# A product of constants in front of the last up-projection part of a two-block transformer kernel

## The chip, the cores and the metric

The kernel runs on one core of one Trainium2 chip. The metric is the device time of one execution in microseconds (us), from the first to the last instruction and a little around it. A program is run several times; the median stands for it.

## What is computed

256 tokens of width 2048 pass through two transformer blocks in float32. Only the second block's last half touches the change:

```python
# first block: stick-breaking attention, then a squared-ReLU MLP (2048 -> 8192 -> 2048)
# second block: chunked attention beside a multi-scale pool, then
h = rms_norm_2(x, pre_ffn_g[l])
up = causal_dwconv(h @ w_up[l], conv_w[l], conv_b[l])          # 2048 -> 2 x 5632
y = (jax.nn.gelu(up[..., :D_FF_2], approximate=True) * up[..., D_FF_2:]) @ w_down[l]
x = x + rms_norm_2(y, post_ffn_g[l])
```

All weight matrices are read once from memory (some 395 MB), and nearly all the work is their products with the 256 tokens.

## The kernel before

**Split operands.** Every float32 operand of a large product is held as two rounded halves, a high one and a low one (fp32r tiles): weights as `Wh` and `Wl`, activations as the first and the second 256 columns of a tile of `aHL`, `oHL1`, `oHL2`, `hid1` or `hid2`. A product is the sum high x high + high x low + low x high.

**Pieces and strips.** The weights come in 746 pieces of 256 rows by 512 columns (512 KB each). SP's queue loads a piece into one of six buffers of `raw`, ACT (ScalarE) rounds it into `Wh` (line 812), DVE (VectorE) makes `Wl = raw - Wh` (line 1024), both into rings of five buffers. Eight to twelve pieces that add up into the same PSUM banks are a strip. Two PSUM sets, `ps0` and `ps1`, of four banks of 512 columns take turns, one strip each.

**Two kinds of pieces**, by what stands still in the PE array (TensorE):

- Kind "T" (`feature_products`, line 1353) gives features by tokens. Weights stand, tokens move. For each of two weight row tiles and four banks it issues a pair: `Wh` against all 512 columns of the activation tile (its high and low halves), and `Wl` against the first 256. A piece is 8 pairs, 16 products, 8 x 768 = 6144 columns.
- Kind "N" (`row_products`, line 1341) gives tokens by features. Tokens stand, weights move. A piece is 12 products of 512 columns, 6144 columns too.

The queries, keys, both up-projections, the first block's output and down projections are T; the values, the second block's output and down projections are N.

**Order.** `plan_program` (line 53) writes one list of steps that all engines walk in order. `strip` (line 83) lists the pieces; `after` puts side jobs behind a certain piece. A step `products` is one piece. The second block's feed-forward runs in two parts, `c = 0` with six strips of each half of the up-projection and `c = 1` with five (loop at line 540): the part's up-projection strips (T), then its down projection `w_down_2` (N, four strips of 12 pieces in part 0 and of 10 in part 1). So part 1's up-projection, 10 strips or 80 pieces, follows directly on an N strip.

**Side products on PE** are few, in plain float32, and put in between pieces: column sums of squares (step `rms`, line 1397, one column each), and after them `spread` (line 1423), which multiplies the 128x128 tile `ones` with a 256-column diagonal tile to give a norm's factor as a row for each partition. ACT copies that row out of PSUM into `r_a` or `r_b` (line 840). Further there are the attention products, `mixed_tiles` (line 1478, sixteen 128-column products that scale and turn four tiles) and transposes. The last norm before the up-projection is `r6`; its row goes into `r_b` during part 0's second strip and is not written again. POOL (GpSimd) multiplies each up-projection strip by `r_b` (line 1314).

**The PE program** (line 1377): for a step `products` it waits for the strip's bank set, the activation tiles and the piece's `Wl` (`s_w_lo`), then issues the piece; every product is issued in `mm`, line 1336, so the profile gives nearly all of them this one line. The lines that are changed are in `strip`, in the loop at line 540 and in the branch at line 1386.

Of the kernel before, what the change touches and what calls it, by code (L numbers as in the profile page):

```python
# [11 lines left out]
TOK = 256  # L12
# [13 lines left out]
class Plan:  # L26
# [18 lines left out]
    def after(self, i, job, ahead=False):  # L45
        jobs = self.later_steps.setdefault(i, [])
        jobs.insert(0 if ahead else len(jobs), job)
# [5 lines left out]
def plan_program(sem):  # L53
    p = Plan(sem)
    step, done, after, later = p.step, p.done, p.after, p.later
    free = {n: [] for n in ("QK1", "T0", "T1", "E", "zs", "set0", "set1", "mT", "qk0", "qk1", "v0", "v1", "A0", "A1")}
    st = {}
# [25 lines left out]
    def strip(w, col, ks, mov, tiles, evac, kind="T", koff=0):  # L83
        first = len(p.pieces)
        for n, kp in enumerate(ks):
            src = (w, "rows", kp * 256, col)
            p.pieces.append(dict(src=src, shape=2, mov=mov, kt=2 * (kp - koff), tiles=tiles, kind=kind, first=n == 0,
                                 last=n == len(ks) - 1, evac=evac))
        return first


# [19 lines left out]
    def rms(name, col):  # L111
        s = side_set()
        total, mean, root = done("rms_total"), done("rms_mean"), done("rms_root")
        rec, sq, prod = done("rms_rec"), done("rms_rec"), done("rms_rec")
        r, diag = done("rms_r"), done("rms_diag")
        step("rms", set=s, col=col, need=st["total"], free=list(free[f"set{s}"]), ones=ones0, ident=ident,
             total=total, mean=mean, root=root, rec=rec, sq=sq, prod=prod, r=r, diag=diag)
        free["zs"], free[f"set{s}"] = [total], [mean]
        st[name + "c"] = r
        st["diag"] = diag  # L120
# [24 lines left out]
    def spread(name, row):  # L145
        s = side_set()
        turned, copied = done("row_turned"), done("row_copied")
        step("spread", set=s, row=row, diag=st["diag"], free=list(free[f"set{s}"]), turned=turned, copied=copied)
        free[f"set{s}"], free["zs"] = [copied], [turned]
        st[name] = copied  # L150

    def r_job(name, col, row):
        def f():
            rms(name, col)
            after(p.at + 1, lambda: spread(name, row), ahead=True)
        return f
# [115 lines left out]
    def evac_relu(t0):  # L272
        def f(s, k):
            summed, kw = common(s, k, free["T1"])
            relu, sq = done("relu_cut"), done("relu_squared")
            hi, lo = done("hid_hi"), done("hid_lo")
            step("relu", t0=t0, r=st["r2"], relu=relu, sq=sq, hi=hi, lo=lo, hid_free=[k], **kw)
            free["T0"], free["T1"] = [lo], [sq]
            hid_tiles[t0:t0 + 4] = [lo] * 4
        return f  # L280
# [11 lines left out]
    for c, n in enumerate((6, 5, 5)):  # L292
        for j in range(n):
            i = strip("mlp_w1", (at + j) * STRIP, ALL8, "aHL", tile_hl, evac_relu(4 * j))
# [156 lines left out]
    def evac_conv(j, which, t0):  # L451
        def f(s, k):
            summed, kw = common(s, k, free["T1"])
            step("sum", **kw)
            name = "E" if which else "zs"

            def scaled():
                u = done("conv_scaled")
                step("conv_scale", need=[summed, st["r6"]], done=u)
                free["T1"] = [u]  # L460
                later(1, lambda: newest(u))

            def newest(u):
                c = [done("conv_newest") for m in range(4)]
                step("conv_newest", which=which, j=j, need=[u, conv_in, *free[name]], c=c)
                free["T1"] = [c[3]]
                later(1, lambda: older(u, c, 0))
                later(2, lambda: older(u, c, 2))
                later(3, lambda: gated(st["older", which]))

            def older(u, c, m0):
                d1 = [done("conv_older") for m in range(2)]
                d2 = [done("conv_older") for m in range(2)]
                step("conv_older", which=which, j=j, m0=m0, c=c, d1=d1, d2=d2)
                st["older", which] = d2[1]
                free["T1"] = [d2[1], c[3]]

            def gated(c):
                if not which:
                    st["gelu"] = done("gelu")  # L480
                    step("gelu", need=c, done=st["gelu"])
                    return
                g = done("gated")
                step("gate", need=[c, st["gelu"]], done=g)
                free["zs"] = [g]

                def halves():
                    hi, lo = done("hid_hi"), done("hid_lo")
                    step("gate_halves", t0=t0, need=[g, k], hi=hi, lo=lo)
                    free["E"] = [lo]  # L490
                    hid_tiles[t0:t0 + 4] = [lo] * 4
                later(1, halves)
            later(0 if "r6" in st else 4, scaled)
        return f
# [45 lines left out]
    for c, n in enumerate((6, 5)):  # L540
        for j in range(n):
            for which in range(2):
                i = strip("w_up_2", which * 5632 + (at + j) * STRIP, ALL8, "aHL", tile_hl, evac_conv(at + j, which, 4 * j))
                if at + j + which == 0:
                    after(i + 10, r_job("r6", "b", "r_b"))
        for s4 in range(4):
            i = strip("w_down_2", s4 * STRIP, tuple(range(2 * at, 2 * (at + n))), "hid2", hid_tiles, evac_y(c, s4), kind="N",
                      koff=2 * at)
            if c == 1 and s4 == 0:
                after(i + 1, gain_rows)  # L550
                after(i + 6, turn_x3(0))
                after(i + 8, turn_x3(1))
                after(i + 12, lambda: step("ready_sqrt", need=None))
        at += n
# [49 lines left out]
    for i in range(N):  # L604
        q = p.pieces[i]
# [41 lines left out]
def build(nc, A, out):  # L647
    with ExitStack() as ctx:
# [14 lines left out]
        ones = sb("ones", [128, 128])  # L663
# [3 lines left out]
        r_b = sb("r_b", [128, TOK])  # L667
# [50 lines left out]
        p = plan_program(lambda name: ctx.enter_context(nc.semaphore(name)))  # L718
# [615 lines left out]
        def tensor_program(e):  # L1334
            def mm(o, l, r, start, stop):
                return e.matmul(o, l, r, start=start, stop=stop, skip_group_check=True)  # L1336
# [16 lines left out]
            def feature_products(q, P, half=None):  # L1353

                wh, wl, mov, kt = Wh[:, q["n"] % NW, :], Wl[:, q["n"] % NW, :], movs[q["mov"]], q["kt"]
                for t in range(2):
                    if half:
                        e.wait_ge(*half[t])
                    x = mov[:, kt + t, :]
                    for m in range(4):  # L1360
                        c = slice(t * 512 + m * 128, t * 512 + (m + 1) * 128)
                        mm(P[:, m, :], wh[:, c], x, q["first"] and t == 0, False)
                        r = mm(P[:, m, 0:TOK], wl[:, c], x[:, 0:TOK], False, q["last"] and t == 1)
                return r
# [12 lines left out]
            for st in p.steps:  # L1377
                k = st["kind"]
                if k == "products":
                    q = pieces[st["i"]]  # L1380
                    P = ps[q["set"]]
                    for t in st["need"]:
                        e.wait_ge(*t)
                    if st["lo"] and not st["half"]:
                        e.wait_ge(*st["lo"])
                    if q["kind"] == "T":
                        feature_products(q, P, (st["half"], st["lo"]) if st["half"] else None).then_inc(p.mm, 1)
                    elif q["kind"] == "P":
                        group_products(q, P).then_inc(p.mm, 1)
                    else:  # L1390
                        for row in st["rows"]:
                            m = row_products(q, row, P)
                            if row == 0 and st["row0"]:
                                m.then_inc(p.row0, 1)
                            if row == 1:
                                m.then_inc(p.mm, 1)
                elif k == "rms":
                    P = ps[st["set"]]
# [7 lines left out]
                elif k == "rms_pair":  # L1406
                    P = ps[st["set"]]
# [20 lines left out]
                elif k == "sb_scores":  # L1428
                    g, P = st["g"], ps[st["set"]]
                    q, kk = qk[:, g % 2, 0, :, :], qk[:, g % 2, 1, :, :]  # L1430
# [7 lines left out]
                elif k == "sb_weights":  # L1438
                    g, P = st["g"], ps[st["set"]]
                    for t in st["need"]:  # L1440
                        e.wait_ge(*t)
                    for b, terms in enumerate((((tri_r, 0),), ((tri_r, 1), (ones_r, 2)), ((tri_r, 2),))):
                        for n, (l, at) in enumerate(terms):
                            c = slice(at * 512, (at + 1) * 512)
# [3 lines left out]
                elif k == "values":  # L1448
                    g, blk, P = st["g"], st["blk"], ps[st["set"]]
# [3 lines left out]
                    for h in range(4):  # L1453
                        c = slice(h * 128, (h + 1) * 128)
# [3 lines left out]
                elif k == "sm_scores":  # L1458
                    g, P = st["g"], ps[st["set"]]
                    q, kk = qk[:, g % 2, 0, :, :], qk[:, g % 2, 1, :, :]  # L1460
# [17 lines left out]
                elif k == "mixed_tiles":  # L1478
                    j0, b0, P = st["j0"], st["b0"], ps[st["set"]]
                    for t in st["need"]:  # L1480
                        e.wait_ge(*t)
                    for n, i in enumerate((0, 2)):
                        for a in range(2):
                            for t in range(2):
                                j = j0 + i + a
# [3 lines left out]
                elif k == "turn_x3":  # L1489
                    c = st["c"]  # L1490
# [63 lines left out]
```

## Time and profile before

| what | value |
|---|---|
| median of 3 runs | 2148.95 us (2148.35 to 2153.14) |
| the profiled execution's own time | 2148.78 us |
| its span, first to last instruction | 2147.0 us |
| PE busy | 2128.6 us, 99% |
| DVE busy | 1286.2 us, 60% |
| ACT busy | 1064.4 us, 50% |
| POOL busy | 242.2 us, 11% |
| read from memory | 395.55 MB, 185 GB/s over the span |

The profiled execution has 1.8 us outside its span. PE's records are of matmuls that overlap in the pipeline, so a busy PE is not PE at its peak: how fast it goes is read from the starts of its records, one after the other.

### The profile page before, as it was taken

What the parts mean: (1) busy time and instruction counts of PE and PEld (TensorE: products, weight loads), DVE (VectorE), ACT (ScalarE), POOL (GpSimd) and SP (SyncE); (2) the same over time, 40 slices, a digit from 0 to 9 for tenths busy, and PEclk for the clock granted to TensorE, in tenths of its full rate; (3) what the DMA queues carried; (4) which work ended last, traced back from release to release, by engine and by line L of the source; (5) the groups of instructions that cost most, each with busy time, mean ns of one, the idle gap of its engine ahead of it and who ended that gap; (6) DMA issues with size and microseconds to landing.
All of it is one profiled execution on the core that took longest, in us unless ns stands there. A gap on an engine that the chain in (4) does not pass through costs nothing.

```text
span 2147.0 us, 28153 instructions
## 1 busy us (share of the span) xinstructions
PE 2128.6 (99%) x11698; PEld 1848.7 (86%) x11698; DVE 1286.2 (60%) x1335; ACT 1064.4 (50%) x1198; POOL 242.2 (11%) x135
## 2 busy tenths in 40 slices
PE   8999999999999999999999999999999999999998
PEld 7888888888888888888888888888888888888886
DVE  6555556655555565565669655576666644566655
ACT  6554554545334443444554544455455433554553
POOL 3000001100000000000224000032222100222211
PEclk9999999999999999999999999999999999999999
DMA  8555555565656655665566555545665666566563
GB/s 279 162 174 174 177 166 187 177 205 167 211 191 183 196 185 192 177 205 189 191 193 193 178 175 181 182 148 179 193 196 177 215 193 189 167 187 202 191 199 113
DMA packets 207472, 399.50 MB, mean 186 GB/s; under 512 B 12400, under 2 KB 15600, under 8 KB 207088
## 3 DMA queue, kind: packets, MB, share of 16 engines
q1 hardware_dynamic: 207056, 395.60, 58.4%
q8 instruction: 92, 1.51, 0.3%
q10 hardware_dynamic: 288, 2.10, 0.3%
q14 instruction: 36, 0.29, 0.0%
HBM read 395.55 MB, written 2.10 MB: 185 GB/s over the span
## 4 chain that ended last, share of the span: by engine, by line
PE 98%; DVE 1%; ACT 0%; DMA 0%; issue 0%; SPq 0%; DVEq 0%; ACTq 0%
PE ps L1336 98%; DMA raw<-in_sb_w_qkv_dram 0%; PE ps L1339 0%; DVE raw L1234 0%; DVE Wl L1024 0%; DVE E L1063 0%; ACT E L862 0%; ACT E L860 0%; ACT T L958 0%; ACT zs L855 0%; DVE QK L1213 0%; ACT E L858 0%; ACT L860 0%; ACT Wh L812 0%; DVE aHL L1186 0%
## 5 line engine op out<-in xcount | busy, mean ns | idle before, releaser
L1024 DVE TENSOR_TENSOR Wl<-raw,Wh 128x1024 fp32r<-128x1024 f32 x745 | 920.4, 1256 | 618.0 <-ACT Wh L812 617.1
L1336 PE MATMUL ps<-aHL,Wh 128*128 128x512 f32 x3328 | 1164.4, 395 | 8.3 <-DVE Wl L1020 6.5
L812 ACT ACTIVATE Wh<-raw 128x1024 fp32r<-128x1024 f32 x745 | 768.6, 1054 | 608.3 <-PE ps L1336 602.9
L1336 PE MATMUL ps<-aHL,Wl 128*128 128x256 f32 x3328 | 931.9, 280 | 0.0
L1336 PEld LDWEIGHTS ps<-aHL,Wh 128*128 128x128 f32 x3328 | 624.7, 188 | 150.7 <-DVE aHL L1014 6.5
L1336 PEld LDWEIGHTS ps<-aHL,Wl 128*128 128x128 f32 x3328 | 629.7, 189 | 0.4
L1336 PE MATMUL ps<-hid,Wh 128*128 128x512 f32 x1024 | 355.1, 391 | 0.0
L1336 PE MATMUL ps<-hid,Wl 128*128 128x256 f32 x1024 | 286.9, 280 | 0.0
L1336 PEld LDWEIGHTS ps<-hid,Wh 128*128 128x128 f32 x1024 | 191.5, 187 | 41.9
L1336 PE MATMUL ps<-Wh,hid 128*128 128x512 f32 x704 | 217.6, 390 | 0.0
L1336 PEld LDWEIGHTS ps<-hid,Wl 128*128 128x128 f32 x1024 | 193.8, 189 | 0.0
L1336 PEld LDWEIGHTS ps<-Wh,hid 128*128 128x128 f32 x704 | 132.2, 188 | 27.4
L1336 PE MATMUL ps<-Wl,hid 128*128 128x512 f32 x352 | 137.0, 389 | 0.0
L1336 PE MATMUL ps<-Wh,aHL 128*128 128x512 f32 x384 | 121.4, 392 | 0.5 <-DVE Wl L1024 0.5
L1261 POOL TENSOR_TENSOR E<-E 128x512 f32<-128x512 f32 x8 | 10.4, 1305 | 943.4 <-ACT E L816 943.4
L1314 POOL TENSOR_TENSOR T<-T,r_b 128x1024 f32<-128x1024 f32 x22 | 71.0, 3229 | 400.2 <-DVE T L979 392.4
L979 DVE TENSOR_TENSOR T<-ps,T 128x1024 f32<-128x1024 f32 x54 | 66.1, 1224 | 56.3 <-ACT T L786 54.8
L1336 PE MATMUL ps<-oHL,Wh 128*128 128x512 f32 x272 | 94.6, 394 | 0.0
L786 ACT ACTIVATE T<-ps 128x1024 f32<-128x1024 f32 x54 | 55.2, 1022 | 68.5 <-PE ps L1336 68.5
L1336 PEld LDWEIGHTS ps<-Wh,aHL 128*128 128x128 f32 x384 | 72.1, 188 | 15.9 <-DVE Wl L1024 0.9
L1336 PE MATMUL ps<-Wh,oHL 128*128 128x512 f32 x256 | 79.6, 390 | 0.0
L1336 PEld LDWEIGHTS ps<-Wl,hid 128*128 128x128 f32 x352 | 66.1, 188 | 13.6
(171 smaller groups left out, 1290.4 us busy)
## 6 DMA issues: line engine op xcount, KB each, us to landing
raw<-in_mlp_w_dram SPq DMA_DIRECT2D x256, 512.0 KB, 4.3
raw<-in_w_up_dram SPq DMA_DIRECT2D x176, 512.0 KB, 3.9
raw<-in_sb_w_qkv_dram SPq DMA_DIRECT2D x95, 512.0 KB, 4.8
raw<-in_w_down_dram SPq DMA_DIRECT2D x88, 512.0 KB, 4.2
raw<-in_w_in_dram SPq DMA_DIRECT2D x64, 512.0 KB, 4.4
raw<-in_sb_w_o_dram SPq DMA_DIRECT2D x32, 512.0 KB, 4.4
raw<-in_w_o_dram SPq DMA_DIRECT2D x32, 512.0 KB, 4.0
xT<-in_x_dram SPq DMA_DIRECT2D x8, 256.0 KB, 7.9
```

The source lines that it names most:

```text
L786: e.activation(T0[:, :, :], ps[st["set"]][:, :, TOK:2 * TOK], ACT.Copy).then_inc(st["copied"][0], 1)
L812: e.activation(Wh[:, i % NW, :], rawv[:, i % NRAW, :], ACT.Copy).then_inc(st["hi"][0], 1)
L979: e.tensor_tensor(T1[:, :, :], ps[st["set"]][:, :, 0:TOK], T0[:, :, :], ALU.add).then_inc(st["summed"][0], 1)
L1024: e.tensor_tensor(Wl[:, i % NW, :], rawv[:, i % NRAW, :], Wh[:, i % NW, :].bitcast(F32), ALU.subtract).then_inc(st["lo"][0], 1)
L1261: e.tensor_tensor(B[:, 0:2, :], B[:, 0:2, :], B[:, 2:4, :], ALU.add).then_inc(st["half"][0], 1)
L1314: e.tensor_tensor(T1[:, :, :], T1[:, :, :], rows4("r_b"), ALU.mult).then_inc(st["done"][0], 1)
L1336: return e.matmul(o, l, r, start=start, stop=stop, skip_group_check=True)
```

## The change

In front of the first piece of part 1's first up-projection strip, PE gets one more product: `ones` (128x128, float32) stands, `r_b` (256 columns, float32) moves, and the result goes to the first 256 columns of bank 0 of the strip's own set. The next product, the strip's first, opens bank 0 anew, so the result is overwritten and nobody reads it. PE also waits there for `r6`, the copy of the factor row into `r_b`.

```diff
@@ strip
             p.pieces.append(dict(src=src, shape=2, mov=mov, kt=2 * (kp - koff), tiles=tiles, kind=kind, first=n == 0,
-                                 last=n == len(ks) - 1, evac=evac))
+                                 last=n == len(ks) - 1, evac=evac, wide=None))
@@ the loop over the parts of the up-projection
                 if at + j + which == 0:
                     after(i + 10, r_job("r6", "b", "r_b"))
+                if c == 1 and j + which == 0:
+                    p.pieces[i]["wide"] = lambda: st["r6"]
@@ tensor_program, step "products"
                     if q["kind"] == "T":
+                        if q["wide"]:
+                            e.wait_ge(*q["wide"]())
+                            mm(P[:, 0, 0:TOK], ones[:, :], r_b[:, :], True, True)
                         feature_products(q, P, (st["half"], st["lo"]) if st["half"] else None).then_inc(p.mm, 1)
```

On PE, where part 0's last down-projection strip (weights `Wh`, `Wl` moving against `hid2`) meets part 1's first up-projection strip (`aHL` moving), there stands before:

```order
9122 L1336 MATMUL ps<-Wl,hid 128x512
9123 L1336 MATMUL ps<-Wh,hid 128x512
9124 L1336 MATMUL ps<-aHL,Wh 128x512
9125 L1336 MATMUL ps<-aHL,Wl 128x256
9126 L1336 MATMUL ps<-aHL,Wh 128x512
```

and with the change, at the same place:

```order
9122 L1338 MATMUL ps<-Wl,hid 128x512
9123 L1338 MATMUL ps<-Wh,hid 128x512
9124 L1338 MATMUL ps<-r_b,ones 128x256
9125 L1338 MATMUL ps<-aHL,Wh 128x512
9126 L1338 MATMUL ps<-aHL,Wl 128x256
```

One row is added and all later ones stand one place further; nothing changes place, on PE or on another engine.

## Rows read from the trace of the kernel before

**Rows 1.** The page: busy time of the engines, PE's granted clock, the chain's shares.

```profile
PE 2128.6 (99%) x11698; PEld 1848.7 (86%) x11698; DVE 1286.2 (60%) x1335; ACT 1064.4 (50%) x1198; POOL 242.2 (11%) x135
...
PEclk9999999999999999999999999999999999999999
...
PE 98%; DVE 1%; ACT 0%; DMA 0%; issue 0%; SPq 0%; DVEq 0%; ACTq 0%
```

**Rows 2.** Who PE waited for from 1390 us on: total us, times, longest us.

```profile
PE ps L1336 <- DVE aHL L1186: 1.3, 1, 1.3
```

**Rows 3.** Stretches: us, PE busy (x records), granted clock, DMA share, GB/s.

```profile
1798.76:2024.88 226.12, 226.12 (x1281) 1.00 0.59 183
...
411.08:1118.05 706.97, 706.97 (x4081) 1.00 0.60 189
...
1435.43:1668.16 232.73, 232.73 (x1344) 1.00 0.60 187
1668.16:1798.76 130.60, 130.60 (x578) 1.00 0.64 201
```

**Rows 4.** PE in order of time at 1798.5 us: start us, us, what.

```profile
1798.54 0.39 PE L1336 MATMUL ps<-Wh,hid 128*128 128x512 f32 x1
1798.76 0.39 PE L1336 MATMUL ps<-aHL,Wh 128*128 128x512 f32 x1
1798.99 0.28 PE L1336 MATMUL ps<-aHL,Wl 128*128 128x256 f32 x1
1799.11 0.40 PE L1336 MATMUL ps<-aHL,Wh 128*128 128x512 f32 x1
1799.34 0.28 PE L1336 MATMUL ps<-aHL,Wl 128*128 128x256 f32 x1
1799.45 0.40 PE L1336 MATMUL ps<-aHL,Wh 128*128 128x512 f32 x1
1799.70 0.28 PE L1336 MATMUL ps<-aHL,Wl 128*128 128x256 f32 x1
1799.82 0.40 PE L1336 MATMUL ps<-aHL,Wh 128*128 128x512 f32 x1
```

**Rows 5.** Shorter stretches of T products, by what stands in front.

```profile
79.90:82.71 2.81, 2.81 (x17) 1.00 0.73 214
1224.77:1227.59 2.82, 2.82 (x18) 1.00 0.88 252
1229.13:1237.36 8.23, 8.23 (x48) 1.00 0.57 161
1409.16:1431.54 22.38, 22.38 (x128) 1.00 0.49 141
1240.21:1273.27 33.06, 33.06 (x193) 1.00 0.60 178
52.05:54.59 2.54, 2.54 (x16) 1.00 0.69 202
...
1125.69:1200.34 74.65, 74.65 (x433) 1.00 0.66 196
...
1119.18:1124.59 5.41, 5.41 (x32) 1.00 0.86 293
```

**Rows 6.** PE in order of time at the last `spread`, 1434.8 us.

```profile
1434.77 0.59 PE L1336 MATMUL ps<-zs,ones 128*128 128x256 f32 x2
1435.01 0.59 PE L1336 MATMUL ps<-aHL,Wh 128*128 128x512 f32 x1
1435.43 0.28 PE L1336 MATMUL ps<-aHL,Wl 128*128 128x256 f32 x1
1435.55 0.39 PE L1336 MATMUL ps<-aHL,Wh 128*128 128x512 f32 x1
1435.78 0.28 PE L1336 MATMUL ps<-aHL,Wl 128*128 128x256 f32 x1
```

**Rows 7.** Tile `r_b`: ACT's copies into it, ns min/median/max, first and last start.

```profile
L840 ACT ACTIVATE r_b<-ps x2: 384/384/384, 411.0 to 1435.4; 128x256 f32<-128x256 f32 x2
```

## The prediction

> **What bounds the kernel now.** I read the page first. PE is busy 99% of the span, the clock it is granted is at the upper of its two levels (2.4 GHz) in all slices, 9 meaning 90% or more, and 98% of the chain that ended last is PE [rows 1]. So a microsecond added to PE's stream or taken from it is a microsecond of the kernel, and nothing else matters unless it makes PE wait. The waits come next: from 1390 us to the end PE waited for another engine once, for 1.3 us, at the start of the up-projection [rows 2]. In the last part PE waits for nobody. What is left to look at is how fast PE's own stream goes when nothing holds it.
>
> For that I cut the trace into stretches in which PE does one kind of piece, with the bounds on the starts of records [rows 3]. A record that is still running at a bound is counted too, so I take the number of products from the program. The last up-projection part is 80 pieces of 8 pairs (512 columns, then 256): 640 pairs in 226.12 us, **353.3 ns a pair**. The up-projection of the part before goes from 1435.43 (the 256-column half of a first pair, 0.12 us) to 1668.16: 671 further pairs in 232.73 - 0.12 = 232.61 us, **346.7 ns a pair**. The long stretch of the first block from 411.08 gives 2039 pairs in 706.85 us, again 346.7 ns. These are the same products on the same tiles, at the same granted clock (1.00), with the same DMA share (0.59 and 0.60), and PE has no gap in either. The same work has two paces, 6.6 ns a pair apart. The starts show what the slow one looks like [rows 4]: from one 512-column product to the next it takes 0.35, 0.34 (or 0.35) and 0.37 us, and so on in threes (1798.76, 1799.11, 1799.45, 1799.82). In the fast one a pair is 0.35 us (its partners at 1435.43 and 1435.78 [rows 6]), and by the mean no long one can come in between.
>
> What chooses the pace? I looked at what PE does right in front of each run of T pieces [rows 5], where a window that opens on a 256-column start has 0.12 us taken off:
>
> - N pieces directly in front: 8 pairs in 2.81 us from 79.90 and 8 in 2.82 us from 1224.77, so 351 and 352 ns, and 353.3 ns over the 640 pairs of the stretch in question, whose first product follows on an N product 0.22 us before [rows 4]. Three other places, at the later query strips of the first block, look like the one at 79.90. The slow pace in 6 of 6.
> - a row `spread` in front (256 columns in plain float32): 7 pairs in 2.42 us from 52.05, 346 ns; 215 pairs in 74.53 us from 1125.69, 346.7 ns; and the two long stretches of [rows 3], 346.7 ns. The fast pace in 4 of 4, also where the T pieces ahead were in the slow pace: 15 pairs in 5.29 us from 1119.18 to the row products before 1125.69, 353 ns.
> - short float32 products in front give either: after transposes 23 pairs in 8.11 us from 1229.13, 353 ns; after `mixed_tiles` 63 pairs in 22.26 us from 1409.16, 353 ns; but after attention values 95 pairs in 32.94 us from 1240.21, 346.7 ns.
>
> No pace changes within a run, the longest being 2040 pairs. So the pace is a steady pattern that the entry picks and that then holds till something else comes between. I read it as a matter of how far the weight loads are ahead of the products when the alternation of 512 and 256 columns begins; a long product in front lets them get ahead. That is a reading, the counts above are what the sum rests on.
>
> **The change part by part.**
>
> 1. *The added product.* It has the form of `spread`: `ones` standing, 256 float32 columns moving. There its two records start at 1434.77, the next T product at 1435.01, and that one's partner at 1435.43 [rows 6]. From the float32 product's start to the partner's start are 0.66 us; without it there would be the usual 0.23 us from a 512-column product to its partner (1435.55 to 1435.78). Price: 0.66 - 0.23 = **0.43 us**, all of it on the path, as PE has no gap here. Bounds: the product can't cost less than nothing. Above, the side work nearest in kind that costs more for its width is the same product's own whole 0.66 us, if nothing of it overlapped. I take 0.43, since form, width and follower are the same; only what is ahead (an N product here, a T product there) and the bank (the follower's own here, another there) differ. The T pairs themselves write one bank twice in a row in every pair, without showing a gap.
> 2. *The added wait.* It is for a copy into `r_b` that was done at 1435.8 [rows 7], more than 360 us before the place. Nothing, and nothing else is queued differently. What is behind it on PE is the whole rest of the program, so I name the cover: it is the 363 us.
> 3. *The pace of the 640 pairs behind it.* At the fast pace they take 640 x 0.3467 = 221.9 us in place of 226.12: **4.24 us less**. The lower bound is no change, 0; the upper bound is this whole difference, since no long stretch of T pieces in the trace is faster than 346.7 ns a pair. I take all of it, because all four 256-column float32 products lead into the fast pace and no stretch in it fell back.
> 4. *What is late next.* Nothing new: the part before ran at the fast pace with the same work on DVE, ACT and POOL and the same loads, and PE did not wait. The down projection behind it is N, 48 pieces in 130.60 us in part 0 [rows 3], 226.7 ns for each of its 576 products; it comes 3.8 us earlier and takes the same time.
>
> Sum: 0.43 - 4.24 = -3.8 us. Against the profiled execution's own 2148.78 us that is 2145.0 us. This execution lies 0.17 us under the median of the runs; from the median it is 2148.95 - 3.8 = **2145.1 us**, 0.18% less. A measurement of this kernel can tell about 0.2% from no change, which is 4.3 us, so the forecast lies just inside that.
>
> Here a rule of the Trainium skill speaks against the change. The trace's row is that the same pairs take 353.3 ns in one stretch and 346.7 in another [rows 3]. The page "TensorE: Matmul & The Clock Gate", section "Wait — 56ns, not 53.3ns?", says that once the array is warm a matmul costs its columns at 2.4 GHz and a fixed 2.5 ns or so, whatever came before it; by it a pair is one number, an estimated 325 ns, there is no pace to choose, and the sum is the added product alone. The trace disagrees with the fixed part: both paces are above it, and they differ from each other.
>
> **The rivals.**
>
> *A. The pace stays slow and the product is only paid for.* The wide product stands behind an N stream here, and in all four cases of the trace behind T pieces, which already alternate. If the pace is set by something that the N stream leaves behind (or by nothing that a single product changes), the 640 pairs stay at 353.3 ns. For it: short float32 products between T pieces leave the slow pace in place twice [rows 5]. Against it: the row products before 1125.69, which turned a slow stretch into a fast one, so a wide product does act on the pattern; and the attention values, which have 256-column products too, lead to the fast pace. Time: 2148.95 + 0.43 = **2149.4 us**, slower than before. It decides from the point at which the gain is under the price: 0.43 us over 640 pairs is 0.7 ns, so if the pair stays above 352.6 ns the change loses. This is also what the page's rule named above would give.
>
> *B. The fast pace comes, but is lost on the way.* At the starts of pieces PE has waits for `Wl`, and a late one could bring the slow pattern back. Against it: three stretches of 215, 671 and 2039 pairs at the fast pace never fell back. If it is lost half way, the gain is 2.1 us less the price, **2147.3 us**.
>
> *C. The change doesn't do what it says.* The instruction stands in PE's stream exactly once and in front of the right strip, so only a product that is shortened away by the hardware would do; nothing in the trace hints at that. Nothing for it beyond what A gives.
>
> **How the numbers follow.** Forecast 0.81, A 0.14, B 0.05. The forecast's own spread is that of medians of a few runs: 2148.35 and 2148.95 are 0.6 us apart, and one of the three runs was 4.2 us above, as much as one such stretch in the other pace, so a median may move by half a microsecond: 2144.3 to 2145.9. To hold 8 in 10 the range has to take in A, with the same slack: 2144.2 to 2149.7. For the signs the bound is 2144.65. The forecast misses it by 0.5 us; I give it a chance of 0.31 that the measurement falls beyond, so faster by over 0.2% is 0.81 x 0.31 = 0.25. Slower by over 0.2% needs a median that caught a disturbed run, 0.04. The rest, 0.71, is within 0.2%.
>
> **What would show it.** In the profile after, two records `r_b,ones` of 256 columns stand at about 1798.8 us, and the first pair's 256-column product starts 0.66 us behind their start. The stretch of T products from there to the first down-projection product is about 222.3 us long in all, in place of 226.12, and the starts of its 512-column products have no third pair of 0.37 us. The last down projection starts at about 2021.1 us in place of 2024.88. PE has no new wait. Everything before 1798 us is as it was. The prediction is wrong if the pairs stay at 353 ns (A), if the first pair comes more than 0.7 us after the product, or if another stretch changes its pace.

## The result and the profile after

| | before | with the change |
|---|---|---|
| median | 2148.98 us (22 runs) | 2145.1 us (22 runs) |
| lowest and highest | 2147.58 to 2154.05 | 2143.79 to 2149.83 |
| ratio, 95% interval | | 0.9982 [0.9976, 0.9988] |

The change gains 3.9 us, 0.18%, where 3.8 us and a time of 2145.1 us were forecast. The profiled execution of the changed kernel doesn't show this gain in its span, because it is one of two among the 22 that lie 4 to 5 us above the rest: it took 2149.53 us, with a span of 2147.8 us. The kernel before has such executions too, four of its 22, from 2152.28 to 2154.05 us.

The page of the kernel after, its span, busy times, granted clock and the chain's shares, answering to [rows 1]:

```profile
span 2147.8 us, 28157 instructions
...
PE 2129.4 (99%) x11700; PEld 1849.0 (86%) x11700; DVE 1285.9 (60%) x1335; ACT 1064.6 (50%) x1198; POOL 241.4 (11%) x135
...
PEclk9999999999999999999999999999999999999999
...
PE 98%; DVE 1%; ACT 0%; DMA 0%; issue 0%; SPq 0%; DVEq 0%; ACTq 0%
```

There are two records more on PE (one float32 product is two) and two weight loads, and else the picture is the same. PE's waits from 1390 us on, as in [rows 2]:

```profile
PE ps L1338 <- DVE aHL L1188: 1.3, 1, 1.3
```

The added wait costs nothing. Now PE in order of time at the added product, kernel after (start us, us, what), to be held against [rows 4] and [rows 6]:

```profile
1803.12 0.39 PE L1338 MATMUL ps<-Wh,hid 128*128 128x512 f32 x1
1803.35 0.59 PE L1338 MATMUL ps<-r_b,ones 128*128 128x256 f32 x2
1803.59 0.59 PE L1338 MATMUL ps<-aHL,Wh 128*128 128x512 f32 x1
1804.01 0.28 PE L1338 MATMUL ps<-aHL,Wl 128*128 128x256 f32 x1
1804.13 0.39 PE L1338 MATMUL ps<-aHL,Wh 128*128 128x512 f32 x1
1804.36 0.28 PE L1338 MATMUL ps<-aHL,Wl 128*128 128x256 f32 x1
1804.48 0.39 PE L1338 MATMUL ps<-aHL,Wh 128*128 128x512 f32 x1
```

From the product's start to the first partner's are 0.66 us, as at the row product of before, and behind it a pair takes 0.35 us. The stretches of the kernel after (us, PE busy, granted clock, DMA share, GB/s), answering to [rows 3]: part 1 from the added product on, the same from the first partner on, part 0 from its first partner on, and part 0's down projection:

```profile
1803.35:2025.65 222.30, 222.30 (x1284) 1.00 0.57 185
1804.01:2025.65 221.64, 221.64 (x1281) 1.00 0.57 185
1435.55:1672.76 237.21, 237.21 (x1345) 1.00 0.57 185
1672.76:1803.35 130.59, 130.59 (x579) 1.00 0.61 200
```

Part 1 takes 222.30 us in place of 226.12: 3.8 us less. Without the first partner's 0.12 us, 639 pairs take 221.52 us, 346.7 ns each. But part 0, which the change does not touch, takes 237.21 us for what took 232.73 before: 671 pairs at 353.3 ns, the slow pace. That is 4.5 us more, and it is why this one execution is not shorter than the profiled one of before. So the trace shows two things at once: the mechanism that was forecast for part 1, and the reason why this execution lies above.

### The profile page after: what moved, and what is told of

It reads as the page before. It is cut to its first block, busy times and chain, and to the rows that moved or that the text cites. A ratio compares the mean times of both kernels' runs of the same rounds, so it can differ in the third digit from the quotient of the medians.

```text
span 2147.8 us, 28157 instructions
## 1 busy us (share of the span) xinstructions
PE 2129.4 (99%) x11700; PEld 1849.0 (86%) x11700; DVE 1285.9 (60%) x1335; ACT 1064.6 (50%) x1198; POOL 241.4 (11%) x135
## 4 chain that ended last, share of the span: by engine, by line
PE 98%; DVE 1%; ACT 0%; DMA 0%; issue 0%; SPq 0%; DVEq 0%; ACTq 0%
PE ps L1338 98%; DMA raw<-in_sb_w_qkv_dram 0%; PE ps L1341 0%; DVE raw L1236 0%; DVE Wl L1026 0%; DVE E L1065 0%; ACT E L864 0%; ACT E L862 0%; ACT T L960 0%; ACT zs L857 0%; DVE QK L1215 0%; ACT E L860 0%; ACT L862 0%; ACT Wh L814 0%; DVE aHL L1188 0%
```

## The experiments

Twelve runs on the chip. Each is the changed kernel with one thing different, unless it says otherwise. The pace in part 1 is read in every profile from the first partner's start to the first down-projection product. It came out as 221.64 or as 225.90 us each time that all 640 pairs were at one pace (225.89 us in the kernel before), never between: 346.7 or 353.3 ns a pair. The executions without a profile have only their time, and a slow part 0 and a slow part 1 each add some 4 us to it, so a single time 4 us above doesn't say which part was slow.

### The change again

> The change once more, for a second profile. Theory L (lead): the T products take the fast pace (346.7 ns a pair) if the weight loads are ahead of the products when the alternation of 512 and 256 columns begins, and a wide float32 product gives that lead unless its own weight load came late. L expects 346.7 ns over the 640 pairs behind the added product, a price of 0.43 us, and in the part before it (672 pairs from 1435 us) 346.7 ns if the row product's weight load was not held up, 353.3 if it was. A span of about 2143.4 us in the first case, 2147.8 in the second. Rival W (width alone): every 256-column float32 product leads into the fast pace; it expects 346.7 in both parts always. Rival D (drift): the pace is drawn at random at each entry; it expects either pace behind the added product in this profile.

Measured: 2145.06 us median (10 runs, 2144.57 to 2146.02), ratio 0.9979 [0.9969, 0.9989]. In this profile both parts have the fast pace, with a span of 2143.1 us (part 0 from its first partner, then part 1 from its own):

```profile
1435.29:1668.04 232.75, 232.75 (x1345) 1.00 0.57 188
1799.29:2020.93 221.64, 221.64 (x1281) 1.00 0.57 186
```

So the 4.5 us of the first profile come and go with part 0's pace, and the profile's span follows: 2147.8 - 2143.1 = 4.7 us. Rival W had fallen with the first profile already, whose part 0 is slow behind a product of 256 columns; D is not excluded by this one.

What was different at part 0's entry in the profile after? There the row product's weight load waited for the diagonal tile from DVE, which was ready late (weight loads of the kernel after: start us, us, what, idle before it and its releaser):

```profile
1434.43 0.19 PEld L1338 LDWEIGHTS ps<-aHL,Wl 128*128 128x128 f32 x1
1434.78 0.30 PEld L1338 LDWEIGHTS ps<-zs,ones 128*128 128x128 f32 x2 [0.16 <-DVE zs L998]
```

In the kernel before these two loads began 0.23 us apart, with no wait:

```profile
1434.42 0.19 PEld L1336 LDWEIGHTS ps<-aHL,Wl 128*128 128x128 f32 x1
1434.65 0.30 PEld L1336 LDWEIGHTS ps<-zs,ones 128*128 128x128 f32 x2
```

Theory L took that for the cause: a wide product gives the weight loads a lead unless its own load is late. But in this second profile the load was held up just so, and the fast pace came all the same:

```profile
1434.52 0.30 PEld L1338 LDWEIGHTS ps<-zs,ones 128*128 128x128 f32 x2 [0.16 <-DVE zs L998]
```

The other profiles say the same. Eleven of the fourteen, before and the experiments below included, have this load held up (the row product's two records start 0.30 to 0.32 us apart, in place of 0.22), and ten of these eleven have a fast part 0. L stood only on one case, and the next runs went for it at the added product.

### The product behind a drained pipeline, and the drain alone

```diff
                         if q["wide"]:
                             e.wait_ge(*q["wide"]())
+                            e.wait_ge(p.mm, q["n"])
                             mm(P[:, 0, 0:TOK], ones[:, :], r_b[:, :], True, True)
```

> The added product as in the change, but PE waits in front of it until its own last N product is complete, so that the added product's weight load starts late and in an empty pipeline. L: the lead is gone or smaller, the 640 pairs take 353.3 ns, and the time is before plus 0.43 us plus the drain of some 0.2 us. W: the width alone counts, 346.7 ns a pair, and the time is that of the change plus 0.2 us, 3.6 us under before. D: either.

Measured: 2145.83 us median (10 runs), ratio 0.9985 [0.9976, 0.9995]. PE in order of time:

```profile
1799.15 0.39 PE L1338 MATMUL ps<-Wh,hid 128*128 128x512 f32 x1
1799.69 0.67 PE L1338 MATMUL ps<-r_b,ones 128*128 128x256 f32 x2
1800.01 0.59 PE L1338 MATMUL ps<-aHL,Wh 128*128 128x512 f32 x1
1800.43 0.28 PE L1338 MATMUL ps<-aHL,Wl 128*128 128x256 f32 x1
```

Part 1 from the first partner on, as a stretch:

```profile
1800.43:2022.07 221.64, 221.64 (x1280) 1.00 0.57 185
```

The product starts 0.54 us behind the last N product in place of 0.23, so its load is late, and the pace is fast. L, as it was written, falls: a late load in front of the wide product does not bring the slow pace. Two of the ten executions lie above, at 2149.58 and 2150.27 us.

The second of the pair waits, and leaves the product out:

```diff
                         if q["wide"]:
-                            e.wait_ge(*q["wide"]())
-                            mm(P[:, 0, 0:TOK], ones[:, :], r_b[:, :], True, True)
+                            e.wait_ge(p.mm, q["n"])
```

> No added product; PE only waits in front of the strip until its last N product is complete. The drain alone costs about what it cost with the product, 2145.8 - 2145.1 = 0.8 us. If an empty pipeline is what resets the pattern, the 640 pairs take 346.7 ns and the time is 4.24 - 0.8 = 3.4 us under before; if it takes the wide float32 product (theory W, which the run with product and wait agreed with), 353.3 ns and 0.8 us over before.

Measured: 2147.65 us median, ratio 0.9990 [0.9981, 1.0000], which stands for nothing, as the ten runs fall into two heaps: 2145.04, 2145.52, 2145.56, 2145.82, 2146.07 and 2149.24, 2149.42, 2149.48, 2149.99, 2150.56. The profile is of the upper heap, with part 0 fast and part 1 slow:

```profile
1798.57 0.39 PE L1338 MATMUL ps<-Wh,hid 128*128 128x512 f32 x1
1799.10 0.47 PE L1338 MATMUL ps<-aHL,Wh 128*128 128x512 f32 x1
1799.41 0.28 PE L1338 MATMUL ps<-aHL,Wl 128*128 128x256 f32 x1
1799.53 0.40 PE L1338 MATMUL ps<-aHL,Wh 128*128 128x512 f32 x1
```

Its part 1 from the first partner on, as a stretch:

```profile
1799.41:2025.31 225.90, 225.90 (x1281) 1.00 0.56 183
```

Neither expectation was right: the same program takes either pace from one execution to the next. Of the upper five, the profiled one had part 1 slow; in the others it may have been part 0. The lower five, though, can only be executions in which part 1 was fast, without any added product: at the slow pace no execution of the kernel before was under 2147.2 us. A restart out of a drained pipeline leaves the choice open. With the product behind the same wait, part 1 was fast in the profile and in at least eight of the ten executions.

### Narrower, and rounded

One 128-column float32 product; one of 256 and one of 512 columns with rounded operands; two of 128; one of 192:

```diff
-                            mm(P[:, 0, 0:TOK], ones[:, :], r_b[:, :], True, True)
+                            mm(P[:, 0, 0:128], ones[:, :], r_b[:, 0:128], True, True)
@@ or, without the wait for r6
+                            mm(P[:, 0, 0:TOK], Wh[:, q["n"] % NW, 0:128], aHL[:, q["kt"], 0:TOK], True, True)
@@ or
+                            mm(P[:, 0, 0:2 * TOK], Wh[:, q["n"] % NW, 0:128], aHL[:, q["kt"], 0:2 * TOK], True, True)
@@ or the first of these lines twice, or with 192 for 128
```

> The added product with 128 columns in place of 256. Short float32 products led to either pace in the trace of before. L: the lead gained over two passes of 128 columns is half; if it is not enough, 353.3 ns a pair and a time of before plus 0.22 us; if enough, 346.7 ns, 0.2 us better than the change, 4.0 us under before. W: 353.3 ns, as the width is missing. A view in which any interruption of the N stream is enough: 346.7 ns.

> In place of the float32 product one of 256 columns with rounded operands (the piece's own Wh block standing, its activation tile moving), into the same bank, without the wait for the row; its sum is overwritten. Price about 0.12 us, one pass. L: a 256-column product of one pass leaves less time than a weight load, so no lead is won, 353.3 ns a pair, 0.1 us slower than before. A view in which only the order of 512 and 256 columns at the entry counts (the pattern starts on a 256 after the N stream): 346.7 ns and 4.1 us under before. W: 353.3 ns, as it is not float32.

> In place of the float32 product one of 512 columns with rounded operands (the piece's own Wh block standing, its whole activation tile moving), as wide in time as one float32 record of 256 columns, 0.22 us. W (float32, two records of two passes): 353.3 ns a pair, 0.2 us over before. If only the length of the record in front of the alternation counts, 346.7 ns and 4.0 us under before; but N products have that length too, and did not do it.

> Two float32 products of 128 columns, one behind the other, in place of one of 256: the same passes and columns in all, 0.43 us, but in records of half the length. If the whole float32 time in front counts: 346.7 ns a pair, first distance from the 512-column product to its partner about 0.42 us, and the time of the change. If the length of the last record counts: 353.3 ns, first distance about 0.31 us as with one of them, and 0.4 us over before.

> The two products of 128 columns once more, timed. The N stream in front has one distance for all its products (226 to 227 ns), so by F the state at this entry is the same in every execution and so is the pace: the fast one as in its profile, all executions at 2145 to 2146 us but for the 1 to 2 of 10 that part 0's entry puts 4 us above. If the pace were drawn at random here, as behind the drained pipeline of the run with the wait alone (5 of 10), about half would lie at 2149.5 us.

> The added product with 192 columns. F: one pace in all executions, which one is open; fast gives 2145.1 - 0.1 = 2145.0 us, slow 2148.95 + 0.3 = 2149.3 us. A view by width says that the limit lies between 128 and 256 columns; a view by the length of all float32 records in front (0.11 x 2 slow, 0.11 x 4 fast, 0.215 x 2 fast) says that it lies between 0.22 and 0.43 us, and 192 columns are 0.32.

| added in front of part 1 | part 1 from the first partner | time |
|---|---|---|
| nothing (before) | 225.89 us | 2149.10 to 2149.22 us beside these |
| 512 columns, rounded | 225.90 us | 2149.22 us (1 run) |
| 256 columns, rounded | 225.90 us | 2149.49 us, ratio 1.0002 [0.9993, 1.0012] |
| 128 columns, float32 | 225.90 us | 2149.47 us, ratio 1.0002 [0.9993, 1.0011] |
| 2 x 128 columns, float32 | 221.64 us, twice | 2145.25 us, ratio 0.9986 [0.9977, 0.9995]; an earlier single run 2147.29 us |
| 192 columns, float32 | 221.64 us | 2145.17 us, ratio 0.9979 [0.9970, 0.9989] |
| 256 columns, float32 | 221.64 us, twice | 2145.06 us, ratio 0.9979 [0.9969, 0.9989] |

The single run of two products of 128 columns, 2147.29 us, lies between the heaps for another reason. Both of its parts have the fast pace, but its granted clock over the first 50 us was 0.97 where it was 1.00 in the second profile of the change, and its part 1 starts 2.6 us later.

The edges of it in the trace, PE in order of time and then part 1 as a stretch: one product of 128 columns, two of them, and one of 192:

```profile
1799.10 0.38 PE L1338 MATMUL ps<-r_b,ones 128*128 128x128 f32 x2
1799.24 0.48 PE L1338 MATMUL ps<-aHL,Wh 128*128 128x512 f32 x1
1799.55 0.28 PE L1338 MATMUL ps<-aHL,Wl 128*128 128x256 f32 x1
...
1799.55:2025.45 225.90, 225.90 (x1280) 1.00 0.56 183
```

```profile
1801.09 0.60 PE L1338 MATMUL ps<-r_b,ones 128*128 128x128 f32 x4
1801.45 0.48 PE L1338 MATMUL ps<-aHL,Wh 128*128 128x512 f32 x1
1801.77 0.28 PE L1338 MATMUL ps<-aHL,Wl 128*128 128x256 f32 x1
...
1801.77:2023.41 221.64, 221.64 (x1280) 1.00 0.57 185
```

```profile
1799.63 0.49 PE L1338 MATMUL ps<-r_b,ones 128*128 128x192 f32 x2
1799.82 0.53 PE L1338 MATMUL ps<-aHL,Wh 128*128 128x512 f32 x1
1800.19 0.28 PE L1338 MATMUL ps<-aHL,Wl 128*128 128x256 f32 x1
...
1800.19:2021.83 221.64, 221.64 (x1280) 1.00 0.57 185
```

Not every interruption of the N stream will do, so the gain is not from the break as such, and neither of the two rounded products did anything. But the width of a single product is not the measure either: two of 128 columns bring the fast pace, and behind them the first pair looks as behind one (0.31 and 0.32 us to the partner). What goes with the outcome here is how much float32 work stands in front altogether. From the starts, up to the first partner and less its usual 0.23 us, it is 0.22 us with 128 columns (1799.10 to 1799.55), which is too little, 0.33 us with 192, 0.45 us with two of 128 and 0.43 us with 256, which are enough.

These runs don't separate the type from the length. The two rounded products took 0.11 and 0.22 us by the same reading, so neither was longer than the float32 product of 128 columns that did nothing either, and a longer run of rounded products was not tried here. The trace of before has one, which [rows 5] leave out: in the first block eight rounded products of the attention, 512 columns each, stand between T pieces in the slow pace (from 79.90 us) and further T pieces. The last of them, the first pair behind, and the 32 pairs up to the next side product as a stretch:

```profile
84.35 0.39 PE L1336 MATMUL ps<-E_lo,tri_r 128*128 128x512 f32 x1
84.58 0.40 PE L1336 MATMUL ps<-aHL,Wh 128*128 128x512 f32 x1
84.81 0.28 PE L1336 MATMUL ps<-aHL,Wl 128*128 128x256 f32 x1
...
84.58:95.67 11.09, 11.09 (x65) 1.00 0.72 233
```

That is 347 ns a pair, the fast pace, behind rounded products alone, and it is so at all four such places in all fourteen profiles. So float32 work is not needed for the fast pace; what sets these rounded products apart from the N pieces, behind which it was always the slow one, stays open.

In all of these that ran ten times the time has one heap and up to two of the ten executions some 4 us above it: 2153.38 and 2154.53 with 128 columns and 2153.36 and 2153.69 with 256 rounded ones, where part 1 is slow anyway, 2149.82 with two of 128, none with 192. With 128 columns or 256 rounded ones none of ten came near 2145 us, so part 1 was slow in every execution. With the others it was fast in at least 19 of 20. So behind an N stream, whose products start 0.22 to 0.23 us apart throughout, the entry left no choice that these runs show.

### Behind T pieces

```diff
-                if c == 1 and j + which == 0:
+                if c == 1 and j == 0 and which == 1:
```

> The added product one strip later, in front of part 1's second up-projection strip, so behind T pieces in the slow pace. The first strip's 64 pairs stay slow (0.42 us more than in the change), the 576 pairs behind should be fast: 2145.5 us. F: since T pieces in front leave the entry open by some ns, a few executions may stay slow here besides those of part 0, more than the 1 to 2 of 10 that lie 4 us above. W (the width alone counts): none more.

Measured: 2145.64 us median (10 runs, one at 2150.32), ratio 0.9986 [0.9977, 0.9995]. The first strip stays slow and the 575 pairs behind the product's first partner are fast, (199.46 - 0.12) / 575 = 346.7 ns:

```profile
1822.56:2022.02 199.46, 199.46 (x1153) 1.00 0.56 185
```

So the product turns a slow stretch into a fast one also from among T pieces. That more executions would stay slow was not seen: one of ten lies above, as with the change itself (two of 22).

### Part 0's entry

Two runs went for the executions that lie above. In the first the column sums for `r6` are made one piece earlier, with the row product in its old place, so that its operand is long ready:

```diff
-    def r_job(name, col, row):
+    def r_job(name, col, row, gap=1):
@@ in it
-            after(p.at + 1, lambda: spread(name, row), ahead=True)
+            after(p.at + gap, lambda: spread(name, row), ahead=True)
@@ the loop over the parts of the up-projection
                 if at + j + which == 0:
-                    after(i + 10, r_job("r6", "b", "r_b"))
+                    after(i + 9, r_job("r6", "b", "r_b", 2))
```

> The change, and the column sums for the factor r6 one piece earlier, its row product where it was, so that its operand has been ready for a piece's time. Theory L for the row product: the pace of the 672 pairs of part 0 is even (230 and 117 ns, 346.7 a pair) whenever the row product's weight load is not held up; the executions that lie 4 to 5 us above the rest (14 of 115 so far, over all kernels) are those in which it was held up and the pairs fell into the slow pace. Expected: in the profile the two float32 records at about 1434.7 us start 0.215 us apart (held up they were 0.32) and the first distance behind them is 0.425; among 16 executions none above 2148; the median as the change's, 2145.1. Rival: the outliers have another cause; then some 2 of 16 lie at 2149 to 2150 all the same.

Measured: 2145.80 us median, 11 runs (ratio 0.9982 [0.9973, 0.9991]), one of them at 2149.71. The two records were no longer held up (0.216 us apart), and yet the first distance, from the first T product to its partner, was 0.418 us and not the expected 0.425, and one execution still lies above. In this profile both parts are fast. PE also waited 1.0 us for the column sums, about the 0.7 us by which this version is slower than the change:

```profile
PE ps L1338 <- DVE T L981: 1.0, 1, 1.0
```

So the held-up load is not the cause, at least not alone. The second run issues the row product twice, for `r6` only:

```diff
@@ the step's entry
-        step("spread", set=s, row=row, diag=st["diag"], free=list(free[f"set{s}"]), turned=turned, copied=copied)
+        step("spread", set=s, row=row, twice=name == "r6", diag=st["diag"], free=list(free[f"set{s}"]), turned=turned, copied=copied)
@@ tensor_program, step "spread"
+                    if st["twice"]:
+                        mm(ps[st["set"]][:, 1, 0:TOK], ones[:, :], D, True, True)
                     mm(ps[st["set"]][:, 1, 0:TOK], ones[:, :], D, True, True).then_inc(st["turned"][0], 1)
```

> The change, and the row product for r6 (in part 0) issued twice, one behind the other, as the pair of row products at 1125 us is (two products, four records), which in all ten profiles so far was followed by a first distance of 0.425 us and the even pattern of 230 and 117 ns. Theory F (fixed state in, fixed pace out): which pace T products take is set by a few nanoseconds at the entry; behind T pieces, whose starts wander by some ns, a single row product leaves 0.417 to 0.426 us and now and then the slow pace, a doubled one always 0.425. F expects a price of 0.43 us, a median of 2145.1 + 0.4 = 2145.5 to 2146.0 us, and no execution 4 us above the rest (single: 1 to 2 of 10). Rival: the executions that lie above have nothing to do with this entry, and 1 to 3 of 17 lie at 2149 to 2151 all the same.

Measured: 2149.80 us median, 11 runs: 2145.43, 2145.96, 2145.97, and eight from 2149.54 to 2152.34. The opposite of what was expected. The profile is of the upper heap. PE at part 0's entry:

```profile
1434.69 1.02 PE L1338 MATMUL ps<-zs,ones 128*128 128x256 f32 x4
1435.37 0.58 PE L1338 MATMUL ps<-aHL,Wh 128*128 128x512 f32 x1
1435.79 0.28 PE L1338 MATMUL ps<-aHL,Wl 128*128 128x256 f32 x1
```

The two stretches of the same profile:

```profile
1804.27:2025.91 221.64, 221.64 (x1281) 1.00 0.57 185
1435.79:1672.98 237.19, 237.19 (x1344) 1.00 0.56 185
```

It shows that part 0's entry can fill the upper heap: an edit there alone moved it from 2 of 22 executions to 8 of 11, and the profile shows part 0 at 353.3 ns a pair, part 1 at 346.7. (The one at 2152.34 us lies higher still; no profile shows why.) It also refutes that more float32 work in front is always better: 0.87 us of it led to the slow pace here, while the same doubled form at 1125 us led to the fast one in all fourteen profiles. Nor does the first distance tell the pace, as this run's expectation had it: by the starts in the trace it was 0.418 us here and 0.420 in the profile after, both slow, and 0.418 in the run before this one and 0.419 in the second profile of the change, both fast.

## Why the prediction was right, point by point

- **Step 1, the product's price.** Taken as 0.66 - 0.23 = 0.43 us; in the profile after it is 1803.35 to 1804.01, again 0.66 us. That an N product stands ahead and that the bank is the follower's own made no difference that the trace shows.
- **Step 2, the wait.** No new wait of PE. Right.
- **Step 3, the pace.** 640 pairs at 346.7 ns were forecast, 346.7 measured in every profile with the product in it, and 222.30 us for the stretch where 222.3 were named. The median gained 3.9 us for a sum of 3.8.
- **Step 4, nothing late next.** The down projection's 130.60 us [rows 3] are 130.59 after, and PE does not wait.
- **The page's rule** (once the array is warm, a matmul in a back-to-back stream costs its columns and a fixed 2.5 ns or so: the Trainium skill, "TensorE: Matmul & The Clock Gate", section "Wait — 56ns, not 53.3ns?") leaves the pairs one pace, which is rival A, 2149.4 us. The runs decide against it for these pairs: the same 640 took 346.7 or 353.3 ns each, at a granted clock of 1.00.
- **Rival A** did not come, with 256 columns. With 128 columns and with 256 rounded ones it did, at 2149.5 us.
- **Rival B** was not seen: the part took 221.64 us or 225.90, nothing between.
- **Rival C** did not come: the two records of the product stand at 1803.35 us, as shown above.
- **The signs.** One of the prediction's own signs of being wrong came: in the profile after, another stretch, part 0, changed its pace, and with it the places named moved; the last down projection starts at 2025.65 us there in place of the forecast 2021.1. In the second profile, with part 0 fast, it starts at 2020.93. The median is right because part 0, by the times, stayed fast in most executions of both kernels.

What was wrong is beside the sum. First, the evidence for step 3, "four 256-column float32 products lead into the fast pace", was read from one execution of before and is no rule behind T pieces: the entry of part 0, which was one of the four, went the other way in the profile after and in most executions with a doubled product. The 2153.14 us among the three runs of before was the hint, and the prediction used it for the spread of the median only. The forecast held because the place of the change is behind an N stream, for which the trace of before had no wide product at all; it was the better place, but that was not known, so that much was luck. The rows also left out the four T strips behind rounded attention products, fast in all cases, which speak against a need for float32. Second, the reading that a long product in front lets the weight loads get ahead did not survive. A late load in front of it changed nothing, a row product that was not held up still left an execution above, and a doubled one made it worse. What holds the pattern stays open.

## What to carry to other kernels

Where PE is the bound and never waits, cut its stream into stretches of the same work and divide time by products: a difference of 2% in the pace of identical products is worth looking for, and it may hang on what stands in front of the stretch. A pace that is picked at the entry and held for hundreds of products can be changed by one cheap product there, but only experiments tell which one. And read the list of single executions before one profile: two heaps 4 us apart mean that one profile shows only one of two behaviours, and a time alone doesn't say which stretch was slow.

## What the runs showed of the hardware

- The same alternation of 512- and 256-column products on the same tiles, at a granted clock of 1.00, runs at exactly two paces, 346.7 and 353.3 ns a pair (221.64 us for the stretch in eight of the twelve profiles that have it whole, the changed kernel and its variants, and 225.90 in four), in steady patterns of starts, and keeps the one it has for up to 2039 pairs.
- Directly behind N pieces it took the slow one in every profile. With one float32 product of 128 columns (0.22 us) or one rounded product (0.11 and 0.22 us) between, still the slow one; with 192 or 256 float32 columns, or two products of 128 (0.33 to 0.45 us), the fast one, in every profile. Behind the attention's eight rounded 512-column products it took the fast one, 347 ns a pair over 32 pairs, in every profile.
- Behind T pieces, one float32 product of 256 columns left either: part 0 at 353.3 ns a pair in the profile after, at 346.7 in the second one of the same program.
- Out of a drained pipeline, by a plain wait for its own last product, at least five of ten executions were fast by their times, and the profiled one was slow. By the starts in the trace the wait costs some 0.4 us (0.54 in place of 0.23 us to the added product, then 0.74 in place of 0.66 to the first partner); the median with wait and product was 0.8 us above the change's.
- Executions 4 to 5 us above the rest, which the kernel before has too (2153.14 among the first three), come, where a profile caught them (2149.53 us with the change, and the doubled row product's), from part 0 in the slow pace. None of before's was caught by a profile.
